# A two-block transformer-like network on one core: order of the high and low products in the feed-forwards' near down blocks

## The reference, cut to what matters

```python
def swiglu_ffn(x, w_in, w_out):
    gate, up = jnp.split(x @ w_in, 2, axis=-1)
    return (jax.nn.silu(gate) * up) @ w_out
...
x = x + 0.5 * swiglu_ffn(rms_norm(x, norm_ffn1[l]), ffn1_w_in[l], ffn1_w_out[l])
```

## Time and profile before

| | |
|---|---|
| median of 3 runs | 1521.01 us (1520.73 to 1521.26) |
| profiled execution | 1521.21 us |
| its span, first to last instruction | 1519.4 us |
| TensorE busy | 1510.9 us (99%), 9480 products |
| TensorE weight loads busy | 1315.8 us (87%), 9480 loads |
| VectorE, ScalarE, GpSimd busy | 1052.7, 776.9, 923.4 us |
| granted TensorE clock, mean of the span | 1.000 |
| DMA | 263.64 MB, mean 174 GB/s |
| products on `hid`, 512 and 256 columns | 1056 each |

### The profile page before, as it was taken

One profiled execution on the slowest core, in us unless ns is written; L12 is line 12 of the kernel. 1 busy time (PEld: TensorE's weight loads), 2 busy tenths in 40 slices (PEclk: granted clock), 3 DMA queues, 4 the chain that ended last, 5 costly groups with the idle time before them and its releaser, 6 DMA issues.

```text
span 1519.4 us, 24540 instructions
## 1 busy us (share of the span) xinstructions
PE 1510.9 (99%) x9480; PEld 1315.8 (87%) x9480; DVE 1052.7 (69%) x1472; ACT 776.9 (51%) x1125; POOL 923.4 (61%) x1092
## 2 busy tenths in 40 slices
PE   9999999999999999999999999999999999999998
PEld 7888888888888888888899888888888887888887
DVE  7966555666986668976587986655466666797664
ACT  6554441123655455455567655456555456665542
POOL 4966520201687677876766687578776673168663
PEclk9999999999999999999999999999999999999999
DMA  8665633222565564665634565565555562346553
GB/s 302 209 196 183 205 99 115 85 79 86 199 212 183 168 215 160 192 205 165 228 126 167 186 210 185 183 215 187 162 189 189 186 207 94 138 156 207 188 165 119
DMA packets 113491, 263.64 MB, mean 174 GB/s; under 512 B 9184, under 2 KB 51296, under 8 KB 113248
## 3 DMA queue, kind: packets, MB, share of 16 engines
q1 hardware_dynamic: 113376, 262.09, 52.5%
HBM read 261.00 MB, written 1.05 MB: 172 GB/s over the span
## 4 chain that ended last, share of the span: by engine, by line
PE 74%; DVE 1%; ACT 0%; issue 0%; DVEq 0%; ACTq 0%
PE ps L1866 40%; PE ps L1867 21%; PE ps L1961 2%; PE ps L1982 2%; PE ps L1898 1%; PE ps L1899 1%; PE ps L1897 1%; PE ps L2434 1%; PE ps L2436 1%; PE ps L2435 1%; PE ps L2387 1%; PE ps L1997 0%; PE ps L1998 0%; PE ps L1996 0%; DVE arena L1812 0%; PE ps L1929 0%
## 5 line engine op out<-in xcount | busy, mean ns | idle before, releaser
L571 POOL TENSOR_TENSOR w_lo<-raw,w_hi 128x256 fp32r<-128x256 f32 x1056 | 902.4, 887 | 475.1 <-ACT w_hi L666 471.6
L1866 PE MATMUL ps<-xn,w_hi 128*128 128x512 f32 x2112 | 741.2, 393 | 0.4 <-POOL w_lo L571 0.2
L1867 PE MATMUL ps<-xn,w_lo 128*128 128x256 f32 x2112 | 591.4, 280 | 0.0
L666 ACT ACTIVATE w_hi<-raw 128x1024 fp32r<-128x1024 f32 (+1 forms) x516 | 475.5, 932 | 186.0 <-PE ps L1867 146.1
L1866 PEld LDWEIGHTS ps<-xn,w_hi 128*128 128x128 f32 x2112 | 395.1, 187 | 90.1 <-issue 0.7
L1867 PEld LDWEIGHTS ps<-xn,w_lo 128*128 128x128 f32 x2112 | 398.9, 189 | 0.2
L1866 PE MATMUL ps<-hid,w_hi 128*128 128x512 f32 x1056 | 379.4, 396 | 0.0
L1105 DVE TENSOR_TENSOR w_lo<-raw,w_hi 128x512 fp32r<-128x512 f32 (+1 forms) x245 | 284.8, 1163 | 32.5 <-ACT w_hi L666 27.6
L1867 PE MATMUL ps<-hid,w_lo 128*128 128x256 f32 x1056 | 297.1, 281 | 0.0
L1866 PEld LDWEIGHTS ps<-hid,w_hi 128*128 128x128 f32 x1056 | 198.4, 188 | 49.4
L1211 DVE TENSOR_TENSOR arena<-ps,low_part 128x512 f32<-128x512 f32 x132 | 90.8, 688 | 202.9 <-ACT low_part L783 202.9
(11 more groups left out here) (345 smaller groups left out, 1305.8 us busy)
## 6 DMA issues: line engine op xcount, KB each, us to landing
raw<-blocks SPq DMA_DIRECT2D x418, 512.0 KB, 3.7
raw<-blocks SPq DMA_DIRECT2D x146, 256.0 KB, 3.5
cst<-consts SPq DMA_DIRECT2D x1, 2358.0 KB, 14.5
x<-x_in SPq DMA_DIRECT2D x4, 256.0 KB, 5.9
out<-x SPq DMA_DIRECT2D x4, 256.0 KB, 3.3
cst<-consts SPq DMA_DIRECT2D x1, 109.0 KB, 2.1
```

Source lines behind the costliest of these rows:

```text
L571: ins = nc.gpsimd.tensor_tensor(w_lo[:, slot(n), piece], raw[:, slot(n), piece], w_hi[:, slot(n), piece], ALU.subtract)
L666: nc.scalar.activation(w_hi[:, slot(n), cols], raw[:, slot(n), cols], ACT.Copy)\
L1866: nc.tensor.matmul(where, hi, both.rearrange("p a t -> p (a t)"), start=opens, stop=False)
L1867: return nc.tensor.matmul(where[:, 0:SEQ], lo, both[:, 0, :], start=False, stop=closes)
```

## The change

In `near_products` the four output tiles d = 0 to 3 were gone through once, each with its high and then its low product. Now they are gone through twice: first the four products with high weight halves (512 columns each), then the four with low halves (256 columns each). The instructions are the same eight, with the same operands, flags and destinations; the semaphore is raised by the last low product, as before. `far_products`, the gate and up tiles and all other users of `three_products` stay as they are.

```diff
--- before.py
+++ after.py
@@ -1935,8 +1935,11 @@
                 n = n0 + near_block(c)
                 pe.wait_ge(lo_ready[slot(n)], nth_split(n))
                 for d in range(NEAR):
-                    wh, wl = (w[:, slot(n), d * P:d * P + P] for w in (w_hi, w_lo))
-                    ins = three_products(ps[:, d, :], wh, wl, hid[:, c, :, :], c == 0, c == NFC - 1)
+                    nc.tensor.matmul(ps[:, d, :], w_hi[:, slot(n), d * P:d * P + P], hid[:, c, :, :].rearrange("p a t -> p (a t)"),
+                                     start=c == 0, stop=False)
+                for d in range(NEAR):
+                    ins = nc.tensor.matmul(ps[:, d, 0:SEQ], w_lo[:, slot(n), d * P:d * P + P], hid[:, c, 0, :],
+                                           start=False, stop=c == NFC - 1)
                 ins.then_inc(used[slot(n)], 1)
 
             def far_products(n0, i):
```

## The result

The changed kernel takes 1529.34 us (median of 4 runs, 1529.03 to 1529.51) against 1521.13 for the kernel before on the same chip: ratio 1.0055, interval 1.0039 to 1.0071. It is slower by 8.2 us where I forecast 4.3 us faster, and outside the range (1514.8 to 1525.0).

What follows compares the result with a forecast made beforehand. TensorE's stream of products was taken as the bound. 117 near blocks at 0.037 us gave 4.3 us off 1521.2 (profiled) or 1521.0 (median), 1516.9 or 1516.7, so 1516.8 us was forecast, range 1514.8 to 1525.0.

Steps and rivals of the forecast that it cites:

- The bound: Whole kernel: TensorE's stream of products sets the end, busy 1510.9 of 1519.4 us, with only a few waits.
- grouping by itself is worth nothing: Near block: by uniform rows, four high and four low products take 1.388 us, so only the 50 ns surcharge can change.
- The stall: Third pair of 117 of 132 near blocks: about 33 ns extra, forecast to go; 0.45 for the stall gone.
- breaks a rhythm: Near block: the stall comes in a fixed rhythm of alternating slots behind gate and up, which the change breaks.
- the sum: Near blocks: 117 blocks gain 0.037 us each, 4.3 us in all; the 15 others gain nothing that counts.
- Rival 2: Gate and up behind the near block: slower rhythm, 0.10 us a step, 11.7 less 4.3 gained, 1528.4 us; chance 0.19.
- what the block leaves behind: Gate and up after each near block: expected to keep the fast pace, still 5.55 us a step.
- the three unstalled first blocks: First near blocks of first, third and fifth feed-forward: different end slots, yet fast pace within two pairs; argued against rival 2.
- A mis-sized term: Near block: to fall from 1.437 to 1.400 us, the middle of 1.397 and 1.404.
- Two at 0.227: New near block: two of its four high products start 0.227 us apart, from 512-column products in `rows_tile`.
- three low at 0.120: New near block: three of its four low products take 0.120 us each, from uniform rows of 256-column products.
- The rule on loads: Weight loads: 107 ns for 128 columns fits under either width, so order is worth nothing; treated as a rival.

Runs made afterwards that it cites:

- HHHLLLLH: Near products of one feed-forward ordered three high, four low, one high, where the kernel before alternates high and low: step 7.053 us against 6.987, gate and up 5.643.
- HHHHLLLLL: Changed kernel's grouped order in one feed-forward, four high then four low, with the last low product made twice: near block 1.535 us, gate and up 5.552.

## Why the prediction was wrong

**Right.** The bound (TensorE's stream, no wait), that nothing but the sequence changes, and that grouping by itself is worth nothing: with both operands at a good place the two orders are 0.05 us apart. The stall did go, as forecast. Whether it went because the change breaks a rhythm, as the sum has it, isn't shown: it also goes with the order kept and `hid` moved by 32 bytes. Rival 2 is what happened, and it was given 0.19: a shorter near block with longer gate and up were its signs, and its price of 1528.4 us was 0.9 under the time. That price came close by luck, two errors that offset each other, 11.7 and -4.3 us where 10.2 and -2.0 were measured, and its reason, a block that ends on four 256-column products, fell: HHHLLLLH doesn't and is slow, HHHHLLLLL ends on five and is fast.

**The step that failed** is the one on what the block leaves behind. The sum took gate and up as fixed at 5.55 us, because "the three unstalled first blocks have other slots at their end than the stalled ones, and they too led into the fast pace within two pairs". Three entries were read as a rule. They all came from one order; with the grouped order 112 of 114 entries led into the slow pace. Measured: +0.091 us a step where the sum had 0, 10.2 us in all, and rival 2 had 0.10. The rows had a warning that I weighed too low: the same instructions ran at two stable paces, and I took the slow one for a peculiarity of the fifth feed-forward's opening, where the trace has it in five of the eleven openings. What chose between the two wasn't known, so a change of order ahead of 114 such stretches couldn't be priced at nothing.

**A mis-sized term.** The near block was to fall to 1.400 and fell to 1.420. "Two at 0.227" and "three low at 0.120" were taken from uniform rows on other operands; on `hid` the high slots became 235, 235, 232 and 240. Half the gain of the block went there: 2.0 us, not 4.3.

**The rule on loads.** The Trainium skill, "TensorE: Matmul & The Clock Gate", section "LDWEIGHTS (loading the stationary operand)", gives the time of a load as its columns over 1.2, 107 ns for 128 columns by my estimate from it. The rest was my inference: that such a load fits under a product of either width, so that the order is worth nothing and the changed kernel takes 1521 us. The trace disagrees with the inference where `xn` and `hid` lie as in the case, by 8.2 us, and agrees where both lie well, with the two orders 0.05 us apart. Whether the loads have a part in the difference, no run shows.

**What stays open.** The mechanism under the two paces. Shown is that moving the operands by 32 bytes changes which paces there are, and that the sequence of products ahead of a stretch changes which one holds; waits and the chunk that is read have no part in it. That the instant of entry is what the sequence changes is argued. The padding moves whatever lies behind it as well: ahead of `xn` also what the other engines read and write there, which wasn't moved by itself. Against a part of theirs speaks that settled steps are alike to 1 ns whatever those engines do meanwhile, and that `xn` at its old place had both paces with the arena at four places. Whether the place counts by itself or against the weights' place wasn't tried: `raw`, `w_hi` and `w_lo` never moved. Nor was the length after which places repeat found; it isn't 32, 64 or 128 bytes.

## What to carry to other kernels

Where TensorE is the bound and never waits, look at the starts of long, uniform stretches of products at full resolution before changing their order: if the same code shows two paces, the placing of the moving operand is worth a few cheap trials (here 32 bytes of padding ahead of each of two operands, 6.6 us), and should come first, since it decides what any change of order will seem to be worth. Judge a reorder by what follows it as well as by its own span. A result like "grouping costs 0.5%" is a result on one layout: with 32 bytes more the changed order was faster than the kernel before by 0.3%, and than the old order in the same layout by 11.5 us (1517.36 against 1528.83, one execution each).

## What the runs showed that I had not expected

- The slow pace takes hold and stays, in the changed kernel: 0.3533 us a pair through whole gate and up tiles, 2% over the fast one, at a granted clock of 1.0 throughout and with no idle time.
- More work at nearly no cost: 17 further products of 117 ns in 17 steps for 0.45 us.
- Settled steps lie on a grid. 6.947, 6.953, 6.960, 6.967, 6.973, 6.987, 7.053 and 7.060 us are whole multiples of 6.67 ns (1042, 1043, 1044, 1045, 1046, 1048, 1058, 1059), and steps that take turns are so in sum, as 6.991 + 7.062.
- Settled steps are alike to 1 ns over 17 in a row, whatever DMA and the other engines do beside them (VectorE is busy for 77.0 us of the fifth feed-forward's window and 96.5 of the third's in the kernel before, both 118.77 us long).
